# The first 128 rows' x too transposed by VectorE and exchanged through HBM ahead of both attentions and the last feed-forward

## The reference, cut to what matters

```python
for layer in range(2):
    h = h + 0.5 * swiglu(rms_norm(h, ln_ffn1[layer]), gate, up, down)     # 1024 -> 2816 -> 1024
    u = rms_norm(h, ln_mix[layer])
    h = h + (diff_attention(u, w_qkv, w_o, ...) if layer == 0
             else swa_sink_attention(u, w_q, b_q, sinks, w_o, b_o, k_band, v_band, ...))
    h = h + 0.5 * swiglu(rms_norm(h, ln_ffn2[layer]), gate, up, down)
    if layer == 0:
        k_band, v_band = shared_kv(h, kv_norm, w_k, b_k, w_v, b_v, ...)
return rms_norm(h, final_norm)
```

## Time and profile before

| what | value |
|---|---|
| runs | 928.05 us median of 3 (927.77 to 928.28) |
| the profiled execution | 927.42 us, of which the span is 925.6 us |
| TensorE busy (PE) | 916.3 us, 99% of the span |
| TensorE weight load (PEld) | 752.3 us |
| VectorE (DVE) | 567.8 us, 61% |
| ScalarE (ACT) | 460.8 us, 50% |
| GpSimd (POOL) | 98.1 us, 11% |
| DMA | 197.61 MB, 213 GB/s over the span |
| granted TensorE clock | 0.998 of full speed (2.4 GHz) |

### The profile page before, as it was taken

One profiled execution on the slowest core, in us unless ns is written; L12 is line 12 of the kernel. 1 busy time (PEld: TensorE's weight loads), 2 busy tenths in 40 slices (PEclk: granted clock), 3 DMA queues, 4 the chain that ended last, 5 costly groups with the idle time before them and its releaser, 6 DMA issues.

```text
span 925.6 us, 11505 instructions
## 1 busy us (share of the span) xinstructions
PE 916.3 (99%) x4259; PEld 752.3 (81%) x4259; DVE 567.8 (61%) x573; ACT 460.8 (50%) x584; POOL 98.1 (11%) x172
## 2 busy tenths in 40 slices
PE   9999999999999999999999999999999999999997
PEld 7888888888878888888888888888876788888885
DVE  6666663664487756665467666654578675766542
ACT  6545543555685545444444545433458554444431
POOL 1000006534311100000004000000040010000000
PEclk9999999999999999999999999999999999999999
DMA  9898677556532788876557788874473188888621
GB/s 312 259 284 246 229 256 224 182 194 215 182 97 86 231 264 263 249 259 221 186 168 240 239 251 250 304 238 177 142 268 97 46 272 248 274 244 285 229 83 47
DMA packets 162558, 197.61 MB, mean 213 GB/s; under 512 B 14361, under 2 KB 133217, under 8 KB 162513
## 3 DMA queue, kind: packets, MB, share of 16 engines
q1 hardware_dynamic: 161552, 196.12, 64.9%
q0 software_dynamic: 512, 0.36, 0.5%
q10 hardware_dynamic: 448, 0.53, 0.2%
HBM read 181.77 MB, written 15.20 MB: 213 GB/s over the span
## 4 chain that ended last, share of the span: by engine, by line
PE 93%; DVE 3%; DMA 1%; issue 1%; ACT 1%; SPq 0%; POOL 0%; POOLq 0%; ACTq 0%
PE bank L461 59%; PE bank L498 19%; PE bank L502 9%; PE bank L518 2%; PE bank L554 1%; PE bank L681 1%; DVE w_lo L1664 1%; PE bank L734 1%; DMA x<-in_x 1%; PE bank L674 0%; ACT h L1449 0%; PE bank L656 0%; PE bank L712 0%; SPq L983 0%; DVE shared L1891 0%
## 5 line engine op out<-in xcount | busy, mean ns | idle before, releaser
L1664 DVE TENSOR_TENSOR w_lo<-raw,w_hi 128x2048 fp32r<-128x2048 f32 x154 | 351.8, 2293 | 190.0 <-ACT w_hi L1292 189.8
L1292 ACT ACTIVATE w_hi<-raw 128x2048 fp32r<-128x2048 f32 x154 | 295.1, 1918 | 200.8 <-PE bank L502 104.8
L461 PE MATMUL bank<-w_hi,xT_hi 128*128 128x512 f32 x816 | 319.1, 391 | 0.0
L461 PE MATMUL bank<-w_hi,xT_lo 128*128 128x512 f32 x816 | 317.6, 389 | 0.0
L461 PE MATMUL bank<-w_lo,xT_hi 128*128 128x512 f32 x816 | 317.6, 389 | 0.0
L461 PEld LDWEIGHTS bank<-w_hi,xT_hi 128*128 128x128 f32 x816 | 153.2, 188 | 32.5 <-issue 0.7
L461 PEld LDWEIGHTS bank<-w_hi,xT_lo 128*128 128x128 f32 x816 | 153.2, 188 | 32.0
L461 PEld LDWEIGHTS bank<-w_lo,xT_hi 128*128 128x128 f32 x816 | 153.2, 188 | 31.3
L498 PE MATMUL bank<-w_hi,hT_hi 128*128 128x512 f32 x348 | 135.7, 390 | 0.0
L498 PE MATMUL bank<-w_lo,hT_hi 128*128 128x512 f32 x348 | 135.4, 389 | 0.0
L502 PE MATMUL bank<-w_hi,hT_lo 128*128 128x512 f32 x348 | 107.2, 389 | 0.0
(11 more groups left out here) (181 smaller groups left out, 595.7 us busy)
## 6 DMA issues: line engine op xcount, KB each, us to landing
raw<-in_ffn_w_down SPq DMA_DIRECT2D x88, 512.0 KB, 5.2
raw<-in_ffn_w_gate SPq DMA_DIRECT2D x86, 512.0 KB, 5.6
raw<-in_ffn_w_up SPq DMA_DIRECT2D x86, 512.0 KB, 6.8
raw<-in_a_w_qkv SPq DMA_DIRECT2D x24, 512.0 KB, 5.4
h_bounce<-silu SPq DMA_DIRECT2D x40, 256.0 KB, 6.5
xn<-h_bounce SPq DMA_DIRECT2D x160, 64.0 KB, 3.6
raw<-in_a_w_o SPq DMA_DIRECT2D x8, 512.0 KB, 3.8
raw<-in_b_w_q SPq DMA_DIRECT2D x8, 512.0 KB, 5.3
```

Of the source, the lines that this page charges most:

```text
L461: mm = nc.tensor.matmul(bank[b][:, :], xs[:, kt, own(pos)], ws[:, slot(u), cols], start=(kt == 0 and i == 0), stop=(kt == KT - 1 and i == 2))
L1292: nc.scalar.activation(w_parts(u)[0], raw[:, slot(u), :], ACT.Copy).then_inc(s_hi, 1)
L1664: nc.vector.tensor_tensor(lo, raw[:, slot(u), :], hi.bitcast(F32), ALU.subtract).then_inc(s_lo, 1)
```

## The change

At three of the five places, `FIRST_MOVES = ["ln_mix_0", "ln_mix_1", "ln_ffn2_1"]`, pos 0's x goes the way of pos 1's. TensorE's eight transposes go there; `residual_turned` is called for pos 0 too, SP gets a `x_moved(name, 0)` ahead of `x_moved(name, 1)`, with an exchange buffer of its own. `ln_ffn2_0` and `kv_norm` keep TensorE's transposes for pos 0.

For all x that comes through HBM (pos 1 everywhere, pos 0 at the three places) gain and split are done on tiles: ScalarE writes each 128 x 128 high part with the gain as its scale, VectorE makes each low part as `landed * gain - hi` in one instruction. That is eight small instructions on each engine for a pos, where before there were two 128 x 512 on ScalarE and four on VectorE.

Three orders change too: in the first attention the last projection unit is split by VectorE ahead of `sub_norm(1, 0)` and TensorE does `wo(3, 0, 0)`, `p_transposes(0, 1, 3)`, `wo(3, 0, 1)`, `values(1, 3)`, with the transposes of x in two halves; in the second attention ScalarE copies the last `p_transposed(1, 1, 3)` ahead of `square(0)`.

```diff
+        FIRST_MOVES = ["ln_mix_0", "ln_mix_1", "ln_ffn2_1"]
...
-                    x_transposes("down", f)
+                    if next_name not in FIRST_MOVES:
+                        x_transposes("down", f)
                     down((8, 9, 10), 1)
...
+                wo(3, 0, 0)
                 p_transposes(0, 1, 3)
-                wo(3, 0, 0)
+                wo(3, 0, 1)
                 values(1, 3)
-                wo(3, 0, 1)
                 wo(0, 1)
-                x_transposes("wo", 0)
+                x_transposes("wo", 0, halves=(0,))
                 wo(1, 1, 0)
                 o_transposes(1, 1)
+                x_transposes("wo", 0, halves=(1,))
...
                 wo(0, 1)
-                x_transposes("wo", 1)
                 turned_values(1, 2)
                 turned_values(1, 3)
...
                     if f and k == 3:
-                        x_moved(name)
+                        if name in FIRST_MOVES:
+                            x_moved(name, 0)
+                        x_moved(name, 1)
...
                         if u == u0 + 3:
-                            x_moved(name)
+                            x_moved(name, 0)
+                            x_moved(name, 1)
...
+            def landed_hi(name, pos, j):
+
+                act.wait_ge(s_x_landed[pos][j], 16 * H_READS * (move_no(name, pos) + 1))
+                for kt in range(4 * j, 4 * j + 4):
+                    nc.scalar.activation(squares(x_parts(name)[0], pos, kt), landed_tile(pos, kt), ACT.Copy,
+                                         scale=gain_column(name, kt)).then_inc(s_land_hi[pos], 1)
...
                 square(0, key)
                 split(u0)
-                x_hi(name, 0, key)
+                if name == "ln_mix_0":
+                    in_sbuf(act, ("gains",))
+                landed_hi(name, 0, 0)
+                landed_hi(name, 0, 1)
                 split(u0 + 1)
...
                 p_transposed(1, 1, 2)
+                p_transposed(1, 1, 3)
                 square(0, ("wo", 1))
-                p_transposed(1, 1, 3)
...
+            def landed_lo(name, pos):
+
+                hi, lo = x_parts(name)
+                for kt in range(KT):
+                    dve.wait_ge(s_land_hi[pos], hi_count(name, pos, kt))
+                    ins = nc.vector.scalar_tensor_tensor(out=squares(lo, pos, kt), in0=landed_tile(pos, kt),
+                                                         scalar=gain_column(name, kt),
+                                                         in1=squares(hi, pos, kt).bitcast(F32),
+                                                         op0=ALU.mult, op1=ALU.subtract)
...
+                    if pos == 0 and key == ("wo", 1):
+                        dve.wait_ge(s_filled, filled["pT", 1, 1, 2 + j, 1])
+                    nc.vector.transpose(x_turned[pos][j].rearrange("p (q t s) -> p t q s", q=4, t=4),
...
             def boundary(key, u_last, u0, name, scale=0.5):
-                residual(key, 0, scale, u_last)
+                residual_turned(key, 0, scale, u_last)
...
-                x_gained(name, 0, key)
                 split(u0)
-                x_lo(name, 0)
+                landed_lo(name, 0)
                 split(u0 + 1)
-                residual_turned(key, scale, u_last)
+                residual_turned(key, 1, scale, u_last)
                 split(u0 + 2)
                 split(u0 + 3)
...
             o_lo(0, 0, 1)
+            split(U_WO_A + 3)
             sub_norm(1, 0)
             combine(1, 3)
-            split(U_WO_A + 3)
```

More of the change, by code:

```diff
@@ L328, in trunk, with move_no, gained_count @@
         MOVES = ["ln_mix_0", "ln_ffn2_0", "kv_norm", "ln_mix_1", "ln_ffn2_1"]
+        FIRST_MOVES = ["ln_mix_0", "ln_mix_1", "ln_ffn2_1"]
+        def move_no(name, pos):
+            return (FIRST_MOVES if pos == 0 else MOVES).index("kv_norm" if name == "ln_ffn1_1" else name)
         def y_count(name, j):
             return 2 * RAW.index(name) + j + 1
+        def gained_count(name, j):
+            return 2 * [n for n in RAW if n not in FIRST_MOVES].index(name) + j + 1
         def gain_of(name, j):
@@ L1570, in next_phase @@
                 o_hi(layer, 1, 1)
-                x_hi(name, 0, ("wo", layer))
+                if name in FIRST_MOVES:
+                    landed_hi(name, 0, 0)
+                    landed_hi(name, 0, 1)
+                else:
+                    x_hi(name, ("wo", layer))
                 split(u_next + 1)
@@ L1670, in lo_part @@
                 nc.vector.tensor_tensor(dst, src, hi.bitcast(F32), ALU.subtract).then_inc(s_read[b], 1)
[L1672 to L1688, removed]
@@ L1702, in residual_turned, with x_gained @@
-            def residual_turned(key, scale, u_last, u_between=None):
-                dve.wait_ge(s_used, u_last + 1)
+            def x_gained(name, key, last=True):
+                for j, b in enumerate(x_banks(0)):
+                    dve.wait_ge(s_filled, filled[("xT", *key, j)])
+                    nc.vector.tensor_tensor(y_of(name, j).rearrange("p (t s) -> p t s", t=4),
+                                            bank[b][:, :].rearrange("p (t s) -> p t s", t=4),
+                                            gain_of(name, j).unsqueeze(2).to_broadcast([P, 4, P]),
+                                            ALU.mult).then_inc(s_read[b] if last else s_y, 1)
@@ L1705, in residual_turned @@
+            def residual_turned(key, pos, scale, u_last, u_between=None):
+                if pos == 0:
+                    dve.wait_ge(s_filled, filled[key])
+                else:
+                    dve.wait_ge(s_used, u_last + 1)
                 for j in range(2):
                     cols = slice(BANK * j, BANK * (j + 1))
-                    nc.vector.scalar_tensor_tensor(out=x[:, 1, cols], in0=bank[acc(1, j)][:, :], scalar=scale,
-                                                   in1=x[:, 1, cols], op0=ALU.mult,
-                                                   op1=ALU.add).then_inc(s_read[acc(1, j)], 1)
@@ L1946, in next_phase @@
                 split(u0)
[L1947 removed]
+                if layer == 0:
+                    x_lo(name)
+                else:
+                    landed_lo(name, 0)
                 split(u0 + 1)
[L1949 removed]
+                residual_turned(("wo", layer), 1, 1.0, u0 - 1)
                 split(u0 + 2)
```

154 lines of the change are left out of this document (81 added, 73 removed).

## The result

The changed kernel takes 932.63 us, median of 5 runs (932.1 to 933.94), against 928.05 for the kernel before: ratio 1.0056, 95% interval 1.0045 to 1.0067. The ratio goes by the means of the runs, 933.01 against 927.85; the medians alone give 1.0049. By them it is slower by 4.6 us. Four of the five runs of the kernel before lie between 927.28 and 928.28 us; the fifth, 1150.44 us, is left out of the ratio and has no trace that would explain it. The forecast, 928.9 within 924.8 to 930.9 and most likely no measurable change, did not come true. The profiled execution took 932.63 us with a span of 930.8; before it was 927.42 and 925.6.

A forecast was written before the change was run, and what follows sets the result against it. TensorE, busy 99% of the span, was taken as the bound. Waits of 2.38 and 2.33 plus 0.1 less 3.94 us spared gave +0.87, so 928.9 us, range 924.8 to 930.9.

The forecast's parts named there:

- The mechanism: Behind pos 0's residual, weight splits queue after the landed tiles; two new TensorE waits eat the 3.94 us gain; chance 0.56.
- 2.38 was forecast: At ln_mix_0, TensorE wants u0+2 at 194.72 but it is ready at 197.10: a wait of 2.38 us.
- Rival 1: The exchange stays hidden behind TensorE's passes and the 3.94 us are won whole: 924.1 us; chance 0.22.
- I take 8.72 for it too: Pos 0's exchange, residual start to both halves in SBUF, takes 8.72 us like pos 1's at ln_mix_0.
- the 2.33 forecast: At ln_mix_1, u0+2 is ready at 677.36 but wanted at 675.03: a TensorE wait of 2.33 us.
- a margin of only 0.06 us: At ln_ffn2_1, u0+2 is ready at 743.54 and wanted at 743.60, so no wait.
- Rival 3: Something else, a landing as slow as when weights flow or a reordering that stalls an attention: 931 or more; chance 0.02.
- I take the other swaps there as nothing: In the first attention, swaps other than the earlier split cost nothing, as the same number of groups of transposes is done.
- The tile: Each 128 x 128 high tile on ScalarE was taken as 0.25 us, four as 1.00 us.
- The 0.20 taken as nearest: The nearest row for ScalarE's tile price: the following instruction starts 0.20 us after a 128 x 128 tile.
- Rival 2: Tiles cost more, at 0.377 us each: +2.4 us, 930.4, slower; decisive above 0.33 us a tile; chance 0.20.
- the wait of `turned_values`: At ln_ffn2_1, the transposes of x and the wait behind them go together, sparing TensorE 1.47 us.

The follow-up runs named there:

- Experiment 3: Changed kernel with split(u0 + 1) moved ahead of pos 0's landed tiles (at ln_ffn2_1 between their two halves): 926.43 us, ratio 0.9986 to the kernel before.
- experiment 14: Changed kernel with 24 small TensorE transposes added in the down projection ahead of ln_mix_1: 934.17 us, a single run.
- experiment 13: Changed kernel with 48 small TensorE transposes added in the down projection ahead of ln_mix_1: 935.2 us, a single run.
- 6: Changed kernel with only ln_mix_1 in FIRST_MOVES, tiles and swapped orders kept: 930.62 us, ratio 1.0029 to the kernel before.
- 7: Changed kernel with only ln_ffn2_1 in FIRST_MOVES, tiles and swapped orders kept: 928.51 us, ratio 1.0011 to the kernel before.
- 9 to 11: Already-met waits among TensorE's first-attention projections: 96 or 32 in the changed kernel, 932.22 and 931.91 us; 96 with split(u0 + 1) earlier and TensorE's old order, 925.28 us.
- 2: Changed kernel with TensorE's old order in the first attention and transposes of x in one piece: 931.37 us, ratio 1.0040 to the kernel before.
- 4: Changed kernel with split(u0 + 1) ahead of the landed tiles and TensorE's old first-attention order: 925.63 us, ratio 0.9982 to the kernel before.
- 8: Version with earlier split(u0 + 1) and TensorE's old first-attention order, plus 24 already-met SyncE waits before pos 0's exchange at ln_mix_1 and ln_ffn2_1: 925.74 us, ratio 0.9978.

## Why the prediction was wrong

**The mechanism was right.** At ln_mix_0 everything came as worked out: residual_turned of pos 1 behind a split, u0+1 a little late, u0+2 late by most of the rest, 2.53 us from start to start where 2.38 was forecast. Experiment 3 shows the cause, a split queued behind the landed tiles, by removing it with the order alone. Rival 1 (the exchange hidden, 924.1) did not happen in this kernel.

**The term that failed: "I take 8.72 for it too".** The landing was taken from one exchange at ln_mix_0 and used at three places. At ln_mix_1 it was 10.56, at ln_ffn2_1 9.56. When the landing was 8.88 at ln_mix_1 (experiment 14) the waits there were 0.88 and 1.31 us, together 2.19, or about 2.5 from start to start, close to the 2.33 forecast; in the changed kernel they are 2.56 and 1.30. So 1.67 us of this place's miss is the late landing. At ln_ffn2_1 the forecast itself noted a margin of only 0.06 us; a landing 0.84 later became a delay of 0.80 (0.64 of it idle), which experiment 13, with 8.72, doesn't have. Together 2.5 us, the larger part of the miss. Rival 3 named "a landing as slow as when weights flow" at a chance of 0.02; a slow landing it was, though no run ties it to weights: what goes with it is the transfer of q8. The chance was far too small for a row read at one place only.

**The step that failed: "I take the other swaps there as nothing".** Counting the groups of transposes overlooked which bank the next pass takes. The wait for `xn` in front of `wo(0, 1)` is 0.88 us, and the place came out at +0.52 instead of -0.3: 0.8 us.

**The tile was mis-sized:** 0.30 us measured, 0.25 taken, which is 0.2 us of the 0.27 missed at ln_mix_0; the landing, 8.85 for 8.72, has the other 0.1. The estimate that the prediction made from the Trainium skill ("VectorE: DVE Perf Modes", "The TRN2 errata"), 0.293 us, agrees with this trace, 1.19 / 4 = 0.298. The sum by it would have been 929.4, so the tile alone does not explain the miss. The 0.20 taken as nearest was read from an accumulator read behind a tile, not from tile to tile. Rival 2, decisive from 0.33 us a tile, was not reached.

**What held:** 24 matmuls fewer, the wait of `turned_values` gone (1.36 us gained up to there, 1.47 forecast), the wait for w_lo in the first attention gone, kv_norm -0.49 for -0.4. The misses are 2.9 (the two late places), 0.8, 0.3 and a start-up 0.2 longer, which no part of the change accounts for, less 0.1 at kv_norm: 4.1 on top of +0.87 gives the 4.95 found between the landmarks.

## What to carry to other kernels

Putting a wait for a DMA into an in-order stream is paid by what is queued behind it: moving one split ahead of the landed tiles turned +0.56% into -0.14%, with not one instruction fewer. The time of a DMA round trip spreads, here from 8.7 to 10.8 us for the same instructions, so read it at every place and leave a margin for the worst one where a chain is close. And before two passes are swapped, list which bank each one fills and who must have read it.

## What the runs showed of the hardware

A 16 KB transfer of the instruction queue q8, 0.93 us long in the changed kernel at ln_mix_1 and 0.9 to 1.8 in all 33 cases, goes with a longer write-and-read-back through HBM when it begins inside it: 0.5 to 2.1 us longer. One that begins before the first write leaves it alone.

Which piece is late goes by where the transfer falls. At +1.7 to +2.6 us behind the residual (experiments 6, 7, 14) it is the first write, which lands after 2.6 to 4.0 us instead of 2.0 (in 7 and 14 the second too, after 3.2 and 3.3). At +3.1 to +4.1 (experiments 9 to 11, and 2, 3, 4 and 8 at ln_mix_1) it is the second write, after 2.8 to 4.4, and one read's issue takes SyncE 0.9 to 2.1 us instead of 0.45. At +4.5 and more the issue of a read is long as well, 1.1 to 2.1 us, and both writes are in time, but for the changed kernel at ln_mix_1, where the second write is late.

At ln_mix_1 the transfer moved by 4 us or more with real TensorE instructions put in (experiments 13 and 14), and by no more than its own scatter with met waits on TensorE or SyncE. That a piece of the exchange stands behind it on the same DMA engine would explain the late writes, but no row shows on which engine each piece ran. That stays open, as do the long issue and why it costs 0.5 us in one exchange and 2.1 in another.
